# Hymba decoder step on one core: the in-chunk scores of the HGRN2 heads, per block of 32 tokens

## The reference, cut to what matters

```python
def _hgrn2_chunk(S, q, k, v, logf):
    b = jnp.cumsum(logf, axis=2)
    inter = jnp.einsum('bhck,bhkv->bhcv', q * jnp.exp(b), S)
    diff = b[:, :, :, None, :] - b[:, :, None, :, :]
    decay = jnp.exp(jnp.where(mask, diff, 0.0)) * mask.astype(diff.dtype)
    A = jnp.einsum('bhtk,bhtsk,bhsk->bhts', q, decay, k)
    intra = jnp.einsum('bhts,bhsv->bhtv', A, v)
    ...
    return S_new, inter + intra
```

## Time and profile before

| | |
|---|---|
| median of 3 runs (lowest to highest) | 2554.12 us (2553.91 to 2554.99) |
| the profiled execution's own time | 2556.64 us |
| its span, first to last instruction | 2555.0 us |
| mean granted TensorE clock | 0.985 |
| TensorE busy | 2463.9 us, 96% |
| VectorE, ScalarE, GpSimd busy | 969.5, 618.9, 283.9 us |
| matmuls of L1 to L5 (L479) | 640 records, 75.7 us busy |
| matmuls of D (L468) | 136 records, 18.7 us busy |
| chain that ended last | TensorE 92%, VectorE 5%, ScalarE 2% |

### The profile page before, as it was taken

One profiled execution on the slowest core, in us unless ns is written; L12 is line 12 of the kernel. 1 busy time (PEld: TensorE's weight loads), 2 busy tenths in 40 slices (PEclk: granted clock), 3 DMA queues, 4 the chain that ended last, 5 costly groups with the idle time before them and its releaser, 6 DMA issues.

```text
span 2555.0 us, 33915 instructions
## 1 busy us (share of the span) xinstructions
PE 2463.9 (96%) x13514; PEld 2212.7 (87%) x13514; DVE 969.5 (38%) x1587; ACT 618.9 (24%) x1149; POOL 283.9 (11%) x276
## 2 busy tenths in 40 slices
PE   5999999999999999999899999999999999999995
PEld 4778877878888888888798998999999999999995
DVE  6665764332121121123765665554211211211224
ACT  4243244222031121122323123232200200200211
POOL 0000001212212222222100000000000000000000
PEclk9999999999999999999999999999999999999998
DMA  5322234434444344444422222142223232222323
GB/s 190 104 94 95 84 100 165 146 124 141 134 146 148 128 143 148 144 160 176 125 104 67 67 66 81 60 152 74 91 83 99 82 98 83 88 93 82 99 82 106
DMA packets 86622, 284.34 MB, mean 111 GB/s; under 512 B 14096, under 2 KB 17296, under 8 KB 86544
## 3 DMA queue, kind: packets, MB, share of 16 engines
q1 hardware_dynamic: 41472, 151.01, 17.7%
q0 software_dynamic: 27648, 100.68, 12.1%
q10 hardware_dynamic: 17424, 31.57, 3.5%
HBM read 171.54 MB, written 111.68 MB: 111 GB/s over the span
## 4 chain that ended last, share of the span: by engine, by line
PE 92%; DVE 5%; ACT 2%; issue 1%; ACTq 1%; DVEq 0%
PE bank L419 28%; PE bank L421 28%; PE bank L420 28%; PE aux L479 3%; PE aux L552 1%; PE aux L468 1%; DVE a_lo L1237 1%; PE aux L508 1%; ACT s_in L617 1%; PE aux L531 1%; PE aux L530 1%; DVE xc L1195 1%; PE aux L484 1%; DVE xy L971 0%; PE aux L432 0%
## 5 line engine op out<-in xcount | busy, mean ns | idle before, releaser
L419 PE MATMUL bank<-a_hi,w_hi 128*128 128x358 f32 (+2 forms) x2560 | 925.5, 362 | 37.6 <-DVE a_lo L1237 20.5
L421 PE MATMUL bank<-a_hi,w_lo 128*128 128x358 f32 (+2 forms) x2560 | 908.7, 355 | 0.0
L420 PE MATMUL bank<-a_lo,w_hi 128*128 128x358 f32 (+2 forms) x2560 | 908.4, 355 | 0.0
L419 PEld LDWEIGHTS bank<-a_hi,w_hi 128*128 128x128 f32 x2560 | 485.8, 190 | 89.9 <-POOL w_lo L374 22.6
L421 PEld LDWEIGHTS bank<-a_hi,w_lo 128*128 128x128 f32 x2560 | 486.5, 190 | 46.2
L420 PEld LDWEIGHTS bank<-a_lo,w_hi 128*128 128x128 f32 x2560 | 486.3, 190 | 45.5 <-issue 1.5
L419 PE MATMUL bank<-b_hi,w_hi 128*128 128x512 f32 (+2 forms) x1280 | 453.2, 354 | 0.0
L420 PE MATMUL bank<-b_lo,w_hi 128*128 128x512 f32 (+2 forms) x1280 | 452.8, 354 | 0.0
L421 PE MATMUL bank<-b_hi,w_lo 128*128 128x512 f32 (+2 forms) x1280 | 452.3, 353 | 0.0
L1324 DVE TENSOR_TENSOR xy<-xy,bank 128x356 f32 (+3 forms) x160 | 94.5, 591 | 564.5 <-PE bank L421 564.5
L374 POOL TENSOR_TENSOR w_lo<-w_st,w_hi 128x1024 fp32r<-128x1024 f32 x74 | 180.2, 2435 | 1034.1 <-ACT w_hi L617 1034.1
(11 more groups left out here) (156 smaller groups left out, 1503.7 us busy)
## 6 DMA issues: line engine op xcount, KB each, us to landing
w_st<-in_wall SPq DMA_DIRECT2D x96, 512.0 KB, 4.2
kept_hi<-w_hi SPq DMA_DIRECT2D x96, 512.0 KB, 4.9
kept_lo<-w_lo SPq DMA_DIRECT2D x96, 512.0 KB, 5.7
w_hi<-kept_hi POOLq DMA_DIRECT2D x96, 512.0 KB, 3.8
w_lo<-kept_lo POOLq DMA_DIRECT2D x96, 512.0 KB, 4.6
xs<-in_xT ACTq DMA_DIRECT2D x8, 536.0 KB, 7.2
xy<-in_xT ACTq DMA_DIRECT2D x8, 536.0 KB, 7.1
xs<-in_xT ACTq DMA_DIRECT2D x16, 256.0 KB, 6.5
```

The costliest lines, as they stand in the source:

```text
L419: pe.matmul(ps, wh, xh, start=(j == 0), stop=False)
L420: pe.matmul(ps, wh, xl, start=False, stop=False)
L421: mm = pe.matmul(ps, wl, xh, start=False, stop=(j == 7))
```

## The change

D and L1 to L5 are multiplied per block of 32 tokens: four matmuls for each chunk instead of one, with 32 columns of k loaded and 32 (D) or 16 (levels) tokens of q streamed, each writing its own 32 partitions of one PSUM bank. The tail is cut into a block of 32 and one of 16. The results go through the masked copies of VectorE into a new compact buffer `near`, 128 x 9 x 32, instead of `attn`. Ahead of L6's copies ScalarE copies the four blocks (six in pass 1) from `near` into `attn`. `mask` shrinks from 576 to 112 columns and is loaded by eight DMAs instead of one in each pass. VectorE clears `near` at each pass start, and in D waits until ScalarE has read `near` of the head before.

```diff
+BLK = 32
+HALF = BLK // 2
...
-    if name[0] == "L":
-        return 1 + (p == 1 and int(name[1]) <= 4)
+    if name == "D" or name[0] == "L":
+        return 1
...
-            mask = sb("mask", [P, P + LEVELS * 64], I32, stack=r)
+            mask = sb("mask", [P, BLK + (DIRECT - 1) * HALF], I32, stack=r)
+            near = sb("near", [P, NCH + 1, BLK], stack=r)
...
+        def blocks(c):
+
+            if c < NCH:
+                return [(BLK * b, BLK) for b in range(CH // BLK)]
+            return [(0, BLK), (BLK, T8 - BLK)]
+
+        def right_halves(buf, s0, n, x):
+
+            return buf[:, s0:s0 + n].rearrange("p (n h x) -> p n h x", h=2, x=x)[:, :, 1, :]
+
+        def tail_parts(lv):
+
+            return blocks(NCH) if lv <= 2 else [(0, TAIL)] if lv <= 4 else []
...
@@ -461,13 +479,13 @@
 
                     for t in range(NT[p]):
                         pe.wait_ge(post, post_no(p, 2, i, t) + 1)
-                    for s, (c, m) in enumerate(chunk_sets(p)):
-                        ps = open_bank(a + s)
-                        for j in range(m):
-                            lo_, hi_ = span(c + j)
-                            mm = pe.matmul(ps[0:rows(c), j * P:j * P + rows(c)], k[:, lo_:hi_], q[:, lo_:hi_],
+                    ps = open_bank(a)
+                    for c in range(NCH + p):
+                        for s0, w in blocks(c):
+                            at = slice(CH * c + s0, CH * c + s0 + w)
+                            mm = pe.matmul(ps[s0:s0 + w, BLK * c:BLK * c + w], k[:, at], q[:, at],
                                            start=True, stop=True)
-                        mm.then_inc(aux_done, 1)
+                    mm.then_inc(aux_done, 1)
...
                         if lv < DIRECT:
-                            mm = pe.matmul(ps[:, 64 * c:64 * c + 64], k[:, CH * c:CH * c + CH], qv[:, c, :, 1, :],
-                                           start=True, stop=True)
+                            for s0, w in blocks(c):
+                                at = CH * c + s0
+                                mm = pe.matmul(ps[s0:s0 + w, HALF * c:HALF * (c + 1)], k[:, at:at + w],
+                                               right_halves(q, at, w, x), start=True, stop=True)
                             continue
...
+                    for s0, w in tail_parts(lv) if p else []:
+                        at = CH * NCH + s0
+                        mm = pe.matmul(ps[s0:s0 + w, HALF * NCH:HALF * NCH + w // 2], k[:, at:at + w],
+                                       right_halves(q, at, w, x), start=True, stop=True)
                     mm.then_inc(aux_done, 1)
-                    if p and lv <= 4:
-                        w = T8 if lv <= 2 else TAIL
-                        q8 = q[:, CH * NCH:CH * NCH + w].rearrange("p (n h x) -> p n h x", h=2, x=x)
-                        pe.matmul(open_bank(a + 1)[0:w, 0:w // 2], k[:, CH * NCH:CH * NCH + w], q8[:, :, 1, :],
-                                  start=True, stop=True).then_inc(aux_done, 1)
...
-                act.dma_start(mask[:, :], mask_d).then_inc(smp_in, 16)
+                for b in range(P // BLK):
+                    r_ = slice(BLK * b, BLK * (b + 1))
+                    act.dma_start(mask[r_, 0:BLK], mask_d[0:BLK, 0:BLK]).then_inc(smp_in, 16)
+                    act.dma_start(mask[r_, BLK:].rearrange("p (l j) -> p l j", j=HALF),
+                                  mask_d[0:BLK, P:P + 64 * (DIRECT - 1)].rearrange(
+                                      "p (l j) -> p l j", j=64)[:, :, 0:HALF]).then_inc(smp_in, 16)
...
+                    if x == BLK:
+                        drained(act, AUX[(p, f"L{DIRECT - 1}", i)])
+                        for c in [NCH] * p + [0]:
+                            nc_ = NCH if c == 0 else 1
+                            for s0, w in blocks(c):
+                                dst = attn[s0:s0 + w, CH * c:CH * c + (CH * NCH if c == 0 else T8)].rearrange(
+                                    "p (c t) -> p c t", c=nc_)
+                                ins = fn(dst[:, :, s0:s0 + w], near[s0:s0 + w, c:c + nc_, 0:w], ACT.Copy)
+                        ins.then_inc(near_read, 1)
                     filled(act, a)
...
+                ps = aux[a % 4]
                 if lv == 0:
-                    for s, (c, m) in enumerate(chunk_sets(p)):
-                        filled(dve, a + s)
-                        r_ = rows(c)
-                        lo_, hi_ = span(c, m)
-                        mk = mask[0:r_, 0:r_].rearrange("p (o t) -> p o t", o=1).broadcast_to([r_, m, r_])
-                        dve.copy_predicated(attn[0:r_, lo_:hi_].rearrange("p (c t) -> p c t", c=m), mk,
-                                            aux[(a + s) % 4][0:r_, 0:m * r_].rearrange(
-                                                "p (c t) -> p c t", c=m)).then_inc(aux_free[(a + s) % 4], 1)
+                    mk = mask[:, 0:BLK].rearrange("p (o t) -> p o t", o=1).broadcast_to([P, NCH, BLK])
+                    ins = dve.copy_predicated(near[:, 0:NCH, :], mk,
+                                              ps[:, 0:BLK * NCH].rearrange("p (c t) -> p c t", t=BLK))
+                    for s0, w in blocks(NCH) if p else []:
+                        ins = dve.copy_predicated(near[s0:s0 + w, NCH, 0:w], mask[s0:s0 + w, 0:w],
+                                                  ps[s0:s0 + w, BLK * NCH:BLK * NCH + w])
+                    ins.then_inc(aux_free[a % 4], 1)
                     return
                 x = 1 << (lv - 1)
-                m0 = P + 64 * (lv - 1)
-                parts = [(a, P, 0, CH * NCH, NCH)]
-                if p and lv <= 4:
-                    w = T8 if lv <= 2 else TAIL
-                    parts.append((a + 1, w, CH * NCH, CH * NCH + w, 1))
-                for u, r_, lo_, hi_, nc_ in parts:
-                    filled(dve, u)
-                    w = (hi_ - lo_) // nc_ // 2
-                    dst = attn[0:r_, lo_:hi_].rearrange("p (c n h x) -> p c n h x", c=nc_, h=2, x=x)[:, :, :, 1, :]
-                    src = aux[u % 4][0:r_, 0:w * nc_].rearrange("p (c n x) -> p c n x", c=nc_, x=x)
-                    mk = mask[0:r_, m0:m0 + w].rearrange("p (o n x) -> p o n x", o=1, x=x)
-                    dve.copy_predicated(dst, mk.broadcast_to([r_, nc_, w // x, x]), src).then_inc(aux_free[u % 4], 1)
+                m0 = BLK + HALF * (lv - 1)
+
+                def put(s0, w, c, nc_, at):
+                    h = min(w, BLK) // 2
+                    dst = near[s0:s0 + w, c:c + nc_, 0:2 * h].rearrange("p c (n h x) -> p c n h x", h=2, x=x)[:, :, :, 1, :]
+                    src = ps[s0:s0 + w, at:at + h * nc_].rearrange("p (c n x) -> p c n x", c=nc_, x=x)
+                    mk = mask[s0:s0 + w, m0:m0 + h].rearrange("p (o n x) -> p o n x", o=1, x=x)
+                    return dve.copy_predicated(dst, mk.broadcast_to([w, nc_, h // x, x]), src)
+
+                ins = put(0, P, 0, NCH, 0)
+                for s0, w in tail_parts(lv) if p else []:
+                    ins = put(s0, w, NCH, 1, HALF * NCH)
+                ins.then_inc(aux_free[a % 4], 1)
...
-                    filled(dve, a + 1 + p)
+                    filled(dve, a)
                     dve.wait_ge(post, post_no(p, 2, i, NT[p] - 1) + 1)
                     tt(q[:, 0:th], q[:, 0:th], f[:, 0:th], ALU.mult).then_inc(level, 1)
+                    if n > 0:
+                        dve.wait_ge(near_read, n)
                     place(p, 0, a)
                 elif name[0] == "L":
                     lv = int(name[1])
                     dve.wait_ge(level, 8 * n + lv)
                     filled(dve, a)
-                    if p and lv <= 4:
-                        filled(dve, a + 1)
...
+                dve.memset(near[:, :, :], 0.0)
                 dve.memset(attn[:, :], 0.0).then_inc(zeroed, 1)
                 dve.wait_ge(zeroed, p + 1)
-                dve.wait_ge(smp_in, 16 * (1 + 4 * p))
+                dve.wait_ge(smp_in, 16 * (8 + 11 * p))
```

More of the change, by code:

```diff
@@ L287, in build @@
         zeroed = sem("zeroed")
+        near_read = sem("near_read")
         spread = sem("spread")
```

## The result

| | before | after |
|---|---|---|
| median (lowest to highest) | 2554.55 us (2553.91 to 2555.38), 4 runs | 2509.74 us (2509.40 to 2511.49), 4 runs |
| ratio after / before | | 0.9826, 95% interval 0.9809 to 0.9843 |
| span of the profiled execution | 2555.0 us | 2507.9 us |
| mean granted clock | 0.985 | 0.985 |

The account below looks back on a forecast made before the run. TensorE, busy 96% of the span, was taken as the bound. Savings of 28.0 us there, less 3.4 (mask loads), 0.4 (spread) and 0.1 (start of pass 0), gave -24.1 us: 2530.0 us, range 2518 to 2545.

Parts of the forecast that it names:

- 64 x 0.016 us: TensorE, each level of pass 0: 64 load-and-matmul records at L6's 0.016 us; with 0.32 us, a piece costs 1.34 us.
- E: Rival, full overlap: with four groups the halves run past each other too, half of 16 ns; -25 us more, 2505; chance 0.06.
- The change of shape: TensorE, each piece: going into and out of narrow matmuls costs 0.32 us, 0.10 before the first and 0.22 behind the last.
- D's wait: TensorE's 2.03 us wait before D in pass 0 hangs on VectorE and ScalarE behind the gate matmuls and stays.
- ScalarE's spread: Four copies per head ahead of L6's, 1.5 us; delays pass 0 by 0 to 0.3 us per head, 0.1 taken, 0.4 in all.
- The mask loads: Start of pass 1: seven more ScalarE issues at 0.485 us add 3.4 us, all of it TensorE idle time.
- VectorE's wait for spad's landing: Start of pass 1: this wait moves by the same 3.4 us as the mask issues and adds nothing more.
- The start of pass 0: The eight mask loads there are covered by VectorE's idle time; 0.1 us taken, 1 us if landing took 4.5 us.
- A: Rival, the clock: a thin D behind its wait lets the clock fall in more heads, +3.4 or +7; 2533 to 2537; chance 0.09.
- B: Rival: each record in the changed pieces costs 25 ns instead of 16, 28.2 us more; 2558.2; chance 0.05.
- C: Rival, slower: neighbouring column groups don't overlap, a record costs 0.031 us, +47 us; 2577; chance 0.04.
- D: Rival, instruction supply: nearly fourfold records make the supply break once per piece, 15 us; 2545; chance 0.07.

Follow-up runs that it names:

- run 2: Changed kernel with another group order per level: L1 one at a time, L2 and L3 two, L4 three then one, L5 four reversed; 2530.10 us.
- run 1: Changed kernel with D and L1 to L5 taking two column groups in turn instead of four; 2527.41 us, ratio 0.9887.
- run 5: Changed kernel with ScalarE's copies out of the compact buffer done twice per head, the second time into a spare buffer; 2515.56 us, ratio 0.9844.
- run 6: On top of run 3, SyncE instead of ScalarE issues mask, smask, h0, spad and the first state in pass 1; 2506.35 us, ratio 0.9806.
- run 9: On top of run 6, VectorE waits for the loads of pass 1 behind its three reciprocals instead of ahead of them; 2499.13 us, ratio 0.9779.
- run 10: On top of run 3, VectorE waits for the loads of pass 1 behind its three reciprocals instead of ahead of them; 2507.00 us, ratio 0.9809.
- run 7: Changed kernel with other load and stream widths and group orders per level, and D one group after the other; scores wrong; 2574.73 us.
- run 3: Changed kernel with the compact mask laid out by the host, loaded by one DMA per pass instead of eight; 2506.26 us, ratio 0.9806.
- run 4: Changed kernel with L1 to L5 loading 128 columns and streaming 64 tokens as before the change, all else kept; 2544.79 us, ratio 0.9960.

## Why the prediction was wrong

The direction was right, that TensorE's stream is what counts was right, and both losses were. One factor of the sum was not, and it carried nearly all of it.

**The term that failed** is "64 x 0.016 us" for a level. The step put 0.016 us per record, L6's price with two column groups, on four groups, with this reason: "the wait is between the halves of one matmul, on the same group, and that stays with four groups". Run 2 shows a wait between any two records on one group, 32 ns, whatever matmul they belong to, and runs 1 and 2 that a second and a third neighbour fill it: 0.0267, 0.0142 and 0.0086 us per record for one, two and four groups. With four groups four loads begin within 20 ns of each other, and the next four 32 ns later; in the prediction's reading each four would hold halves that wait for each other, so it can't be right. The trace doesn't say which group a load is for, but pairs that are one record on each of two groups fit: they, too, start 32 ns apart. The chance for E, 0.06, was taken down by this reading of the pairs alone; the rows would have borne "two at a time, because there are two groups" just as well.

Put right, that term closes the balance: 3136 records x (0.016 - 0.0086) = 23.2 us, and 28.0 + 23.2 = 51.2 against 52.2 measured in these pieces. Most of the last 1.0 is the clock in head 1, where D gained 1.4 more than in head 0, less 0.5 behind L5 of head 0.

**The change of shape**, 0.32 us per piece, was taken over and not tested by itself. The burst alone agrees with it: 0.74 us less 0.18 for the last matmul, by 63 steps, is 0.0089 us per record, against 0.0086 with the 0.32 taken off the piece.

**D's wait** stayed at 2.03 us, as said, and D was done 1.07 us sooner instead of 0.62, by the same factor.

**ScalarE's spread** took 1.67 us instead of 1.5, and KT's piece costs 0.01 to 0.05 us more. Taken was 0.1 per head, within bounds of 0 to 0.3. That the slack was used up is shown by run 5.

**The mask loads** at the start of pass 1: 3.4 forecast for the issues, 3.4 measured; 0.5 was missed because the state load behind them took longer to issue. "VectorE's wait for spad's landing moves by the same amount and adds nothing more" was right, and runs 6, 9 and 10 show how near a bound of its own it is. The start of pass 0 came out 0.2 longer against 0.1, which says little: among the traces of all these kernels the same matmul there starts anywhere from 42.1 to 43.8 us.

**The rivals.** A: stretches of low clock moved (head 1 lost one, head 2 kept one), the mean stayed at 0.985; not borne out. B and C: refuted by the price of a record. D: the instruction packets rose by a third, and 15 us were not there. The one wait of 0.51 us without a releaser, which comes back in every kernel with four groups in turn throughout, is what might be left of D; runs 1, 2 and 7 have as many packets and no such wait, so packets alone don't make it, and the cause stays open. E's price, half of 16 ns, is what happened: 2505 forecast for it, 2509.7 measured. Its reason, that the halves run past each other, is not: on one group they keep their 32 ns.

The range stopped at 2518 because only E's near side was taken into it. E's place, 25 us below the forecast, was further than anything that the bounds of the other terms reached.

## What to carry to other kernels

When small fp32 matmuls can be cut by output partitions, issue them so that all four column groups take turns; that order alone was worth 17.7 us here. When a row shows a price at two units in turn, ask which resource is held for how long before carrying it to four. And when the trace names one engine as the cause of a wait, look for a second chain from the same source: removing the first alone, and the second alone, each gave nothing, and both together gave 7 us.

## What the runs showed of the hardware

- A column group of 32 takes an fp32 record every 32 ns (32 columns loaded, 16 or 32 tokens streamed), every 25 ns with 16 and 16, every 56 ns with 64 streamed (run 7). Groups work side by side, loads and streams both: 0.0267, 0.0142, 0.0086 us per record with 1, 2, 4 groups, and 0.0467, 0.0250, 0.0142 with 64 tokens streamed. The Trainium skill, "TensorEngine Tiling (Array Packing)", theoretical speedup, allows four times for 32 columns; 3.1 and 3.3 times were measured over whole pieces, in which the single-group burst already gains from its handovers. By the spacing of loads alone it is four times: four start every 32 ns in L1 of the changed kernel, one in L1 of run 2.
- Which groups are neighbours made no difference, nor did their order (L2, L3 and L5 of run 2).
- Loading 16 instead of 32 columns saved nothing with 64 tokens streamed, and 0.006 us per record with 16.
- A fall of the clock behind D's wait costs 1.4 to 1.6 us up to L1, most of it in dense steps of 0.43 us instead of 0.23 (runs 6 and 3, in all four heads one had the fall and the other not). Where it lies over the narrow burst, that is slower too: in head 2 its loads start over 0.84 us in run 6 and over 0.56 in run 3. It came to other heads in nearly every kernel.
- Equal waits were followed by low clock in one kernel and by full clock in another (run 4 and the change), some 8 us in all. It was not found out what decides.
- TensorE stood still for 0.45 to 0.75 us without a releaser behind L5 of head 0 in all seven kernels in which all levels take four groups in turn, and in none of the other five. The cause was not found.
